# Moving the gate jobs of ScalarE, the gate stores and the gate loads in a two-layer transformer trunk

## The chip, the cores and the metric

The kernel runs on one core of a Trainium2 chip. The metric is the device time of one launch in microseconds (us); before the change it is 4043.3 us, the median of three runs (4035.92 to 4045.26).

## The reference

Two identical layers run one after the other on 512 tokens of width 1024: four sequence mixers and an output projection, a cross-attention to 256 memory tokens, and PEER, a mixture of 16384 tiny experts. The change touches PEER alone:

```python
q = (h @ w_query).reshape(B, L, PEER_HEADS, 2, PEER_HALF)
s = einsum('blhtd,htnd->blhtn', q, sub_keys)             # 8 heads, two sets of 128 keys
s1, i1 = top_k(s[..., 0, :], 16); s2, i2 = top_k(s[..., 1, :], 16)
top_s, pos = top_k(all 256 sums s1 + s2, 16)              # 16 experts per head: 128 per token
idx = i1 * 128 + i2 of those;  gate = softmax(top_s)
a = gelu(einsum('tkd,td->tk', u_tab[idx], h))
out = einsum('tk,tkd->td', gate * a, v_tab[idx])
```

## The kernel before

Each layer first runs the mixers, the cross-attention and the PEER scores; then `peer_experts` does the experts. The first 128 tokens (tile 0) gather their own rows of the two tables by indirect DMA. For the other 384 tokens (tiles t = 1, 2, 3) the kernel computes all 16384 experts densely, in 128 chunks of 128 experts, and multiplies by a gate matrix that is zero except where an expert was chosen. There are two loops over the chunks.

**The u loop** runs over chunks n = 0 to 127. SP loads the 512 KB of u for chunk n (`load_u`, three slots, ahead by the semaphore `u_split`). ScalarE rounds it to a high part (`round_u`, L1748), GpSimd makes the low part (`split_u`, L1844). TensorE multiplies (`experts`, L2076, 24 matmuls into one of two PSUM banks). ScalarE applies gelu (`gelu`, L1758), and in the same routine rounds u of chunk n+3 and stores the result of chunk n-1 to the DRAM tensor `acts` on its own DMA queue (`store_act`, L1752).

**The gates** of a tile t are made inside this loop, in the 16 chunks from START[t] = 34, 69, 104; these chunks are called spread chunks here. VectorE first routes the tile (`route(t)`: the top-k searches, with dot products of tile 0 filled in). Then come 32 jobs of four tokens, two jobs in each chunk. For a job VectorE makes two one-hot matrices (L2009, L2010, L2012, two buffers), TensorE multiplies them (`spread`, L2088, two PSUM banks in turn), and ScalarE copies the bank into an SBUF stage (`evict`, L1780). In a spread chunk TensorE's order is job, half of the 24 expert matmuls, job, the other half. Before job n it waits until ScalarE has copied job n-2 (`staged`). ScalarE copies both jobs of a chunk behind that chunk's `gelu`, so behind the end of its expert matmuls. VectorE makes the matrices of job n only when TensorE is done with job n-2 (`g_done`). TensorE starts chunk START[t]-1 only when the routing of tile t has ended (`sel_ready`).

The stage has two halves of 32 tokens. Each half is stored to the DRAM tensor `gates` in eight pieces of 16 chunks, 512 KB each (`store_gates`, L1769), which ScalarE issues on its DMA queue: those of half 0 at every second job in the second half of the 16 chunks, those of half 1 one per chunk behind them. As a partition holds 64 tokens of a chunk side by side and `gates` is laid out by chunk, a piece is 2048 runs of 256 bytes.

The dot products of tile 0 take their rows from six slots, which GpSimd fills by indirect DMA (`gather_row`, L1850, 512 KB each) between its `split_u` instructions, at chunks that a small planner (`gather_after`) writes out by hand.

**The v loop** runs over the same chunks again: SP loads v (512 KB), `acts` and `gates` (192 KB each) for a chunk, four slots each. VectorE multiplies act by gate (`gate`, L2027), ScalarE rounds (L1794, L1790), VectorE makes the low parts (L2032, L2037), TensorE does 18 matmuls into six banks (L2111). VectorE also adds up the gathered values of tile 0 (L2045, L2048), which GpSimd gathers into the space of stage half 1 (L1857) once the last stores of that half have landed. The first eight chunks are written out, the others run in a loop of eight chunks a turn.

Of the kernel before, what the change touches and what calls it, by code (L numbers as in the profile page):

```python
# [29 lines left out]
P = 128  # L30
# [1535 lines left out]
def peer_experts(k, hh_, hl_, scores, gates, acts, ring):  # L1566
# [16 lines left out]
    RING = 4  # L1583
    BODY = 8
# [5 lines left out]
    v_loaded, act_loaded, g_loaded = k.sems[41:45], k.sems[45:49], k.sems[49:53]  # L1590
    row_got, value_got = k.sems[53:59], k.sems[59:67]
    with ExitStack() as c:
        def sb(name, shape, dt=F32):
# [20 lines left out]
        a_in, g_in = (stages[:, 0, half_v + n * RING * SEQ:half_v + (n + 1) * RING * SEQ].rearrange("p (r t) -> p r t", r=RING)[:, :, 0:DENSE]  # L1614
                      for n in range(2))
# [22 lines left out]
        def job(t, q):  # L1638

            return (t - 1) * JOBS + q  # L1640
# [42 lines left out]

        with nc.Block() as block:
            @block.sync
            def _(e):
# [4 lines left out]
                def load_u(n):  # L1691
                    if n >= 2 + U_SLOTS:
                        e.wait_ge(u_split, n - U_SLOTS - 1)
                    e.dma_start(u[:, n % U_SLOTS, :, :], ut[n]).then_inc(u_loaded[n % U_SLOTS], 16)
# [5 lines left out]
                def load_gated(turn, n):  # L1700
                    s, at = n % RING, turn * BODY + n
                    e.dma_start(a_in[:, s, :], acts[bass.ds(at, 1)].rearrange("o p n -> p (o n)")).then_inc(act_loaded[s], 16)  # L1702
                    e.dma_start(g_in[:, s, :], gates[bass.ds(at, 1)].rearrange("o p n -> p (o n)")).then_inc(g_loaded[s], 16)

                def chunk(turn, n):
                    at = turn * BODY + n
                    e.wait_ge(v_split, at - RING + 1)
                    load_value(turn, n)
                    e.wait_ge(act_split, at - RING + 1)
                    load_gated(turn, n)  # L1710
# [7 lines left out]
                for n in range(5, NKEY):  # L1718
                    for t in (2, 3):
                        if n == (20 if t == 2 else START[3] - 30):  # L1720
                            e.wait_ge(sel_ready, 1 if t == 2 else 3)
                            load_scores(t)
                    load_u(n)
                e.wait_ge(stored[0], 16 * (PIECES - 1) * (TT - 1))
# [3 lines left out]
                e.wait_ge(stored_first[1], 16 * (TT - 1))  # L1728
                for n in range(RING):
                    e.wait_ge(a_stored[n], 16)  # L1730
                    load_gated(0, n)
# [3 lines left out]
                for n in range(RING, BODY):  # L1735
                    chunk(0, n)
                with e.Fori(0, TURNS - 1) as turn:
                    for n in range(BODY):
                        chunk(turn, BODY + n)

            @block.scalar
            def _(e):
# [20 lines left out]

                def store_gates(t, half, piece):

                    some = slice(piece * NKEY // PIECES, (piece + 1) * NKEY // PIECES)
                    at = (t - 1) * P + half * HALF
                    e.wait_ge(staged, job(t, 0) + (half + 1) * JOBS // 2)
                    e.dma_start(gates[some, :, at:at + HALF].rearrange("c p t -> p c t"),  # L1769
                                stage[half][:, some, :]).then_inc(stored[half] if piece else stored_first[half], 16)  # L1770
# [32 lines left out]
                for n in range(NKEY):  # L1803
                    if n == NKEY - 2:
                        e.wait_ge(dotted, KK)
                        e.activation(weights[:, :], dots[:, :], ACT.Gelu_apprx_tanh).then_inc(raised, 1)
                    gelu(n)
                    if n == 12:
                        exp_gates(0)
                    for t in range(1, TT):  # L1810
                        if n == START[t] - 5:
                            exp_gates(t)
                        for q in range(JOBS):
                            if START[t] + (STEPS * (q + 1) - 1) // KT == n:
                                evict(t, q)
                                if q >= JOBS // 2 and q % 2 == 1:
                                    store_gates(t, 0, (q - JOBS // 2) // 2)
                        piece = n - START[t] - JOBS * STEPS // KT
                        if 0 <= piece < PIECES:
                            store_gates(t, 1, piece)  # L1820
                    if n >= NKEY - 2:
                        round_value(0, n - NKEY + 2)
# [57 lines left out]
            def _(e):  # L1880
# [142 lines left out]
                def gate(n):  # L2023
                    s = n % RING
                    e.wait_ge(act_loaded[s], landed(0, n))
                    e.wait_ge(g_loaded[s], landed(0, n))  # L2026
                    e.tensor_tensor(a_in[:, s, :], a_in[:, s, :], g_in[:, s, :], ALU.mult).then_inc(gated, 1)  # L2027
# [239 lines left out]
def scratch_of(nc):  # L2267
    return {n: nc.dram_tensor(n, shape, F32).ap() for n, shape in
            (("scores", (TT, P, 2 * PH, NKEY)), ("gates", (NKEY, NKEY, SEQ - P)), ("acts", (NKEY, P, SEQ - P)), ("memory", (P, KT, MEM)))}
# [73 lines left out]
```

## Time and profile before

| | |
|---|---|
| median of the runs | 4043.3 us |
| the profiled execution | 4064.89 us, span 4063.1 us |
| TensorE busy, matmuls (17778) | 3636.7 us, 90% |
| VectorE / GpSimd / ScalarE busy | 2637.9 / 1658.2 / 1403.6 us |
| mean granted TensorE clock | 0.943 of full speed |
| DMA | 858.49 MB, mean 211 GB/s |

The profile is one execution, so it is compared with its own time; the median of the runs is 21.6 us below it. The span is cut into 40 slices of some 100 us. In layer 0 the u loop runs from about 680 to 1496 us and the v loop from there to 2033 us; in layer 1 from about 2697 to 3515 us and to 4054 us. The matmul engine's digits are 7 to 9 nearly everywhere; inside the u loop they change between 9 and 7.

### The profile page before, as it was taken

The numbers are of one execution on the slowest core, as the hardware profiler recorded it, in microseconds if no ns is written. First come the engines' busy times: TensorE is split into PE (matmuls) and PEld (weight loads), VectorE is DVE, ScalarE is ACT, GpSimd is POOL, SyncE is SP. The second block draws the span as 40 slices with busy tenths as digits, with TensorE's granted clock in tenths as the row PEclk, the third lists the DMA queues.
The fourth block names the chain that finished last, engine by engine and source line by source line (L and its number), as shares of the span: only waits on it lengthen the run. The fifth ranks groups of instructions, "written<-read, shape, count | busy, mean of one in ns | idle before, by whom it ended". The sixth has DMA issues, their size and how long they took to land. (4 is left out here: it accounts for less than half of the span.)

```text
span 4063.1 us, 52955 instructions
## 1 busy us (share of the span) xinstructions
PE 3636.7 (90%) x17778; PEld 3158.1 (78%) x17778; DVE 2637.9 (65%) x5262; ACT 1403.6 (35%) x2400; POOL 1658.2 (41%) x1144
## 2 busy tenths in 40 slices
PE   7888999978879779999988899999788887899999
PEld 6467778978879778888873778789788787788887
DVE  7755512867768638888787544148676675388887
ACT  4254433322323223333332543333223232233332
POOL 4623334644646332222156143447455464322221
PEclk8999999988989889999999899999899898999999
DMA  4004225757769589999731132358487686899996
GB/s 138 25 24 136 68 81 174 255 176 235 270 198 310 180 257 389 353 354 354 258 108 33 42 112 65 85 182 276 164 253 247 202 288 196 282 375 354 354 352 245
DMA packets 513025, 858.49 MB, mean 211 GB/s; under 512 B 236577, under 2 KB 340385, under 8 KB 509345
## 3 DMA queue, kind: packets, MB, share of 16 engines
q1 hardware_dynamic: 204064, 486.56, 36.7%
q0 software_dynamic: 73728, 268.47, 17.2%
q10 hardware_dynamic: 235008, 100.69, 9.0%
q8 instruction: 114, 1.87, 0.2%
q14 instruction: 111, 0.90, 0.1%
HBM read 743.37 MB, written 112.20 MB: 211 GB/s over the span
## 5 line engine op out<-in xcount | busy, mean ns | idle before, releaser
L1844 POOL TENSOR_TENSOR t_ul<-t_u,t_uh 128x1024 fp32r<-128x1024 f32 x168 | 405.5, 2414 | 453.7 <-ACT t_uh L1748 453.1
L1857 POOL DMA_INDIRECT t_stages<-in_peer_v,t_idx x256 | 261.3, 1021 | 749.5 <-DVE pair L2048 702.1
L2076 PE MATMUL pair<-h_high,t_uh 128*128 128x384 f32 x1376 | 508.7, 370 | 44.2 <-ACT t_act L1758 24.2
L1758 ACT ACTIVATE t_act<-pair 128x384 f32<-128x384 f32 x256 | 125.8, 491 | 1133.5 <-PE pair L2076 1049.8
L2111 PE MATMUL pair<-t_v_early,t_ah 128*128 128x512 f32 x1536 | 478.2, 393 | 26.8 <-DVE t_v_early L2037 26.8
L2076 PE MATMUL pair<-h_low,t_uh 128*128 128x384 f32 x1376 | 492.8, 358 | 0.0
L2076 PE MATMUL pair<-h_high,t_ul 128*128 128x384 f32 x1376 | 491.3, 357 | 0.0
L2111 PE MATMUL pair<-h_high,t_ah 128*128 128x512 f32 x1536 | 472.8, 389 | 0.0
L2088 PE MATMUL pair<-t_second,t_first 128*128 128x128 f32 x1536 | 232.8, 299 | 181.1 <-ACT t_stages L1780 181.1
L2009 DVE TENSOR_TENSOR t_second<-iota,pair 128x512 f32<-128x512 f32 x192 | 131.9, 687 | 374.0 <-PE pair L2088 337.3
L2088 PEld LDWEIGHTS pair<-t_second,t_first 128*128 128x128 f32 x1536 | 211.4, 207 | 209.9 <-ACT t_stages L1780 209.9
L2111 PEld LDWEIGHTS pair<-t_v_early,t_ah 128*128 128x128 f32 x1536 | 290.9, 190 | 89.9 <-issue 29.4
L297 POOL TENSOR_TENSOR x_w_low<-x_w_raw,x_w_high 128x512 fp32r<-128x512 f32 x128 | 176.3, 1385 | 438.5 <-ACT x_w_high L290 233.2
L1900 DVE CUSTOM_DVE_ANT_0 t_rows<-t_rows,pair 128x1024 f32<-128x1024 f32 x256 | 308.8, 1211 | 52.6 <-DMA t_rows<-in_peer_rows,t_idx 52.6
L2111 PEld LDWEIGHTS pair<-h_high,t_ah 128*128 128x128 f32 x1536 | 288.3, 188 | 59.9
L2048 DVE SCALAR_TENSOR_TENSOR pair<-t_stages,t_weights,pair 128x1024 f32<-128x1024 f32 x254 | 325.3, 1281 | 0.0
L2076 PEld LDWEIGHTS pair<-h_high,t_uh 128*128 128x128 f32 x1376 | 285.1, 207 | 50.4 <-issue 43.2
L1844 POOL TENSOR_TENSOR h_low<-t_u,h_high 128x1024 fp32r<-128x1024 f32 x84 | 200.5, 2387 | 280.1 <-ACT h_high L1748 279.7
L2111 PE MATMUL pair<-t_v_early,t_al 128*128 128x512 f32 x768 | 301.3, 392 | 0.0
L2111 PE MATMUL pair<-h_high,t_al 128*128 128x512 f32 x768 | 298.8, 389 | 0.0
L2076 PEld LDWEIGHTS pair<-h_low,t_uh 128*128 128x128 f32 x1376 | 284.6, 207 | 0.0
L2076 PEld LDWEIGHTS pair<-h_high,t_ul 128*128 128x128 f32 x1376 | 283.0, 206 | 0.0
(425 smaller groups left out, 8216.2 us busy)
## 6 DMA issues: line engine op xcount, KB each, us to landing
t_u<-in_peer_u SPq DMA_DIRECT2D x256, 512.0 KB, 4.3
t_stages<-in_peer_v SPq DMA_DIRECT2D x256, 512.0 KB, 5.3
acts<-t_act ACTq DMA_DIRECT2D x256, 192.0 KB, 4.3
gates<-t_stages ACTq DMA_DIRECT2D x96, 512.0 KB, 7.4
t_stages<-acts SPq DMA_DIRECT2D x256, 192.0 KB, 5.3
t_stages<-gates SPq DMA_DIRECT2D x256, 192.0 KB, 5.6
p_w_raw<-in_peer_wq SPq DMA_DIRECT2D x64, 256.0 KB, 3.0
m_w_raw<-in_w_in SPq DMA_DIRECT2D x48, 256.0 KB, 2.7
```

Source lines behind the costliest of these rows:

```text
L297: e.tensor_tensor(self.low[:, i % self.SPLIT, 0:width], self.raw[:, i % self.RAW, 0:width], self.high[:, i % self.SPLIT, 0:width].bitcast( ...
L1758: e.activation(act[:, n % A_SLOTS, :], k.bank[n % 2][:, 0:DENSE], ACT.Gelu_apprx_tanh).then_inc(gelu_done, 1)
L1844: e.tensor_tensor(ul[n % U_SLOTS], u[:, n % U_SLOTS, :, :], uh[n % U_SLOTS].bitcast(F32), ALU.subtract).then_inc(u_split, 1)
L1857: e.indirect_dma_start(value_slot[j % V_SLOTS], None, v_rows, bass.IndirectOffsetOnAxis(ap=idx[:, j:j + 1], axis=0)).then_inc(value_got[j ...
L1900: e.tensor_tensor_reduce(out=slot, in0=slot, in1=h_own, scale=1.0, scalar=0.0, op0=ALU.mult, op1=ALU.add, accum_out=dots[:, j:j + 1]).then ...
L2009: e.tensor_tensor(second[:, s, :, :], keys, bcast(selT[1][:, some], 2, NKEY), ALU.is_equal).then_inc(second_ready, 1)
L2048: e.scalar_tensor_tensor(out=own_sum, in0=slot, scalar=w, in1=own_sum, op0=ALU.mult, op1=ALU.add).then_inc(added, 1)
L2076: mm = e.matmul(out, a[n % U_SLOTS][:, q, :], b[:, 1:TT, q, :], start=(q == 0 and m == 0), stop=(q == KT - 1 and m == 2))
L2088: mm = e.matmul(g_bank(n)[:, a * NKEY:(a + 1) * NKEY], first[:, q % 2, a, :], second[:, q % 2, a, :], start=True, stop=True)
L2111: mm = e.matmul(k.bank[2 * t + half][:, :], l[:, s, (t - 1) * P:t * P], r[s][:, half * 512:(half + 1) * 512], start=(begins and m == 0), s ...
```

## The change

- **ScalarE's order.** In a spread chunk the copies of the chunk's two jobs (`evict`) come ahead of its `gelu` instead of behind it. The chunk in which a job is copied is the same.
- **The gate stores** move from ScalarE's to SP's DMA queue, between the u loads. `store_after` says behind which u load a piece goes out: half 0 at START[t]+13 to START[t]+20, one per load; half 1 from START[t]+21 on, one at every second load, for t = 3 two per load.
- **The layout of `gates`** in DRAM becomes (32, 128, 1536): four chunks lie side by side for each partition, so that a piece is 512 runs of 1 KB.
- **The gate loads** of the v loop fetch four chunks at once (768 KB, 6 KB per partition) into one of two buffers. One buffer lies in the stage, the other in the u slots, free once the u loop is done with them. `gate` reads its chunk from there in six runs of 64 elements.

The core of the diff:

```diff
-                    e.dma_start(g_in[:, s, :], gates[bass.ds(at, 1)].rearrange("o p n -> p (o n)")).then_inc(g_loaded[s], 16)
+                def load_gates(turn, g):
+                    at = turn * (BODY // GROUP) + g
+                    e.dma_start(g_store[g % 2], gates[bass.ds(at, 1)].rearrange("o p n -> p (o n)")).then_inc(g_loaded[g % 2], 16)
+        def store_after(t, half, piece):
+            if half == 0:
+                return START[t] + 13 + piece
+            return START[t] + 21 + (2 * piece if t < TT - 1 else piece // 2)
...
-                def chunk(turn, n):
+                def chunk(turn, n, regroup):
                     at = turn * BODY + n
                     e.wait_ge(v_split, at - RING + 1)
                     load_value(turn, n)
                     e.wait_ge(act_split, at - RING + 1)
-                    load_gated(turn, n)
+                    load_act(turn, n)
+                    if n % GROUP == 0 and regroup:
+                        e.wait_ge(gated, at - GROUP)
+                        load_gates(turn, n // GROUP)
...
                     load_u(n)
+                    for t in range(1, TT):
+                        for half in range(2):
+                            for piece in range(PIECES):
+                                if n == store_after(t, half, piece):
+                                    store_gates(t, half, piece)
+                for piece in range(PIECES):
+                    if store_after(TT - 1, 1, piece) >= NKEY:
+                        store_gates(TT - 1, 1, piece)
...
                 e.wait_ge(stored_first[1], 16 * (TT - 1))
+                load_gates(0, 0)
                 for n in range(RING):
                     e.wait_ge(a_stored[n], 16)
-                    load_gated(0, n)
+                    load_act(0, n)
+                e.wait_ge(u_split, NKEY - 2)
+                load_gates(0, 1)
...
+                    for t in range(1, TT):
+                        for q in range(JOBS):
+                            if START[t] + STEPS * q // KT == n:
+                                evict(t, q)
                     gelu(n)
...
-                        for q in range(JOBS):
-                            if START[t] + (STEPS * (q + 1) - 1) // KT == n:
-                                evict(t, q)
-                                if q >= JOBS // 2 and q % 2 == 1:
-                                    store_gates(t, 0, (q - JOBS // 2) // 2)
-                        piece = n - START[t] - JOBS * STEPS // KT
-                        if 0 <= piece < PIECES:
-                            store_gates(t, 1, piece)
```

## Rows read from the trace of the kernel before

**Rows 1.** Who waited for ScalarE's copies, L1780: us, times.
```profile
  PE pair L2088: 181.1, 90
```
**Rows 2.** Timeline of ScalarE, first 16 spread chunks: start, duration, idle before.
```profile
845.53 0.49 ACT L1758 ACTIVATE t_act<-pair 128x384 f32<-128x384 f32 x1 [4.51 <-PE pair L2076]
845.92 1.05 ACT L1748 ACTIVATE t_uh<-t_u 128x1024 fp32r<-128x1024 f32 x1
...
988.07 0.49 ACT L1758 ACTIVATE t_act<-pair 128x384 f32<-128x384 f32 x1 [7.39 <-PE pair L2076]
...
992.23 0.49 ACT L1758 ACTIVATE t_act<-pair 128x384 f32<-128x384 f32 x1 [1.75 <-PE pair L2076]
```
**Rows 3.** The same around chunk 69, the first spread chunk of tile 2.
```profile
1075.15 0.49 ACT L1758 ACTIVATE t_act<-pair 128x384 f32<-128x384 f32 x1 [3.08 <-PE pair L2076]
...
1081.10 0.49 ACT L1758 ACTIVATE t_act<-pair 128x384 f32<-128x384 f32 x1 [4.51 <-PE pair L2076]
```
**Rows 4.** ScalarE and its queue behind spread chunks, layer 0, tiles 1 and 3.
```profile
996.39 0.49 ACT L1758 ACTIVATE t_act<-pair 128x384 f32<-128x384 f32 x1 [2.72 <-PE pair L2076]
996.49 4.34 ACTq L1752 DMA_DIRECT2D acts<-t_act  x1
...
1041.51 0.49 ACT L1758 ACTIVATE t_act<-pair 128x384 f32<-128x384 f32 x1 [0.82 <-PE pair L2076]
...
1476.15 0.49 ACT L1758 ACTIVATE t_act<-pair 128x384 f32<-128x384 f32 x1 [2.72 <-PE pair L2076]
...
1496.42 0.47 ACT L1758 ACTIVATE t_act<-pair 128x384 f32<-128x384 f32 x1
```
**Rows 5.** Stretches: length, busy PE, PEld, DVE, ACT, POOL, clock, DMA share, GB/s.
```profile
845.50:922.00 76.50, 59.29 (x320) 56.73 (x320) 44.73 (x74) 20.36 (x34) 29.34 (x19) 0.87 0.45 154
922.00:988.00 66.00, 53.03 (x281) 51.11 (x282) 41.62 (x105) 15.79 (x27) 26.02 (x17) 0.84 0.73 215
996.00:1041.00 45.00, 39.93 (x218) 38.69 (x217) 42.90 (x152) 12.96 (x18) 29.74 (x20) 0.96 1.09 354
...
1497.00:1560.00 63.00, 52.24 (x219) 42.26 (x220) 45.45 (x55) 22.51 (x30) 21.65 (x21) 0.92 0.99 370
1560.00:1990.00 430.00, 430.00 (x1899) 356.06 (x1898) 357.56 (x427) 156.18 (x212) 109.34 (x107) 1.00 1.00 358
```
**Rows 6.** DMA issues from 996 to 1041 us: count, KB, median us to landing.
```profile
t_u<-in_peer_u SPq DMA_DIRECT2D x9, 512.0 KB, 6.4
gates<-t_stages ACTq DMA_DIRECT2D x7, 512.0 KB, 7.9
...
t_rows<-in_peer_rows,t_idx POOLq DMA_INDIRECT x10, 7.1
```
**Rows 7.** The page's costliest groups: busy us, mean ns, idle before and releaser.
```profile
L1844 POOL TENSOR_TENSOR t_ul<-t_u,t_uh 128x1024 fp32r<-128x1024 f32 x168 | 405.5, 2414 | 453.7 <-ACT t_uh L1748 453.1
...
L2009 DVE TENSOR_TENSOR t_second<-iota,pair 128x512 f32<-128x512 f32 x192 | 131.9, 687 | 374.0 <-PE pair L2088 337.3
...
L1900 DVE CUSTOM_DVE_ANT_0 t_rows<-t_rows,pair 128x1024 f32<-128x1024 f32 x256 | 308.8, 1211 | 52.6 <-DMA t_rows<-in_peer_rows,t_idx 52.6
```
**Rows 8.** Timeline of VectorE: the routing of tile 2, and what follows it.
```profile
979.13 3.19 DVE L1918 MAX8 t_best<-t_s 128x8 f32<-128x128 f32 x16
...
1061.32 0.29 DVE L1992 TENSOR_REDUCE t_esum<-t_ex 128x8 f32<-128x128 f32 x1 [3.06 <-ACT t_ex L1786]
...
1061.88 0.32 DVE L1997 TENSOR_TENSOR t_sel<-t_ex,t_esum 128x128 f32<-128x128 f32 x1
1070.96 0.69 DVE L2009 TENSOR_TENSOR t_second<-iota,pair 128x512 f32<-128x512 f32 x1 [8.76 <-PE pair L2097]
```
**Rows 9.** First and last matmul of the v loop, layer 0; GpSimd's first value gather.
```profile
1503.09 1.19 PE L2111 MATMUL pair<-t_v_early,t_ah 128*128 128x512 f32 x2 [8.51 <-DVE t_v_early L2037]
...
2032.47 0.39 PE L2111 MATMUL pair<-h_high,t_al 128*128 128x512 f32 x1
...
1502.65 1.12 POOL L1857 DMA_INDIRECT t_stages<-in_peer_v,t_idx  x1 [17.05 <-DMA gates<-t_stages]
```
**Rows 10.** The page's DMA issues: the gate loads of the v loop.
```profile
t_stages<-gates SPq DMA_DIRECT2D x256, 192.0 KB, 5.6
```

More of the change, by code:

```diff
@@ L1583, in peer_experts @@
     RING = 4
+    GROUP = 4
     BODY = 8
@@ L1589, in peer_experts @@
     dotted, raised, weighed, added, chunk_done, bank_done, v_round, v_split, gated, act_round, act_split, base_loaded = k.sems[29:41]
-    v_loaded, act_loaded, g_loaded = k.sems[41:45], k.sems[45:49], k.sems[49:53]
+    v_loaded, act_loaded, g_loaded = k.sems[41:45], k.sems[45:49], k.sems[49:51]
     row_got, value_got = k.sems[53:59], k.sems[59:67]
@@ L1613, in peer_experts @@
         v = stages[:, 0, 0:half_v].rearrange("p (r d) -> p r d", r=RING)
-        a_in, g_in = (stages[:, 0, half_v + n * RING * SEQ:half_v + (n + 1) * RING * SEQ].rearrange("p (r t) -> p r t", r=RING)[:, :, 0:DENSE]
-                      for n in range(2))
+        a_in = stages[:, 0, half_v:half_v + RING * DENSE].rearrange("p (r t) -> p r t", r=RING)
+        g_store = [stages[:, 0, half_v + RING * DENSE:half_v + (RING + GROUP) * DENSE],
+                   ring[0][:, :, :, :].rearrange("p r k n -> p (r k n)")[:, 0:GROUP * DENSE]]
+        g_in = [store.rearrange("p (s c t) -> p s c t", s=2 * (TT - 1), c=GROUP) for store in g_store]
+        gate_rows = gates.rearrange("g p (s x) -> g p s x", s=2 * (TT - 1))
         with ExitStack() as until_values:
@@ L1698, in load_value, with load_act, store_gates @@
                      .then_inc(v_loaded[n % RING], 16)
-                def load_gated(turn, n):
+                def load_act(turn, n):
                     s, at = n % RING, turn * BODY + n
                     e.dma_start(a_in[:, s, :], acts[bass.ds(at, 1)].rearrange("o p n -> p (o n)")).then_inc(act_loaded[s], 16)
-                    e.dma_start(g_in[:, s, :], gates[bass.ds(at, 1)].rearrange("o p n -> p (o n)")).then_inc(g_loaded[s], 16)
-                def chunk(turn, n):
+                def load_gates(turn, g):
+                    at = turn * (BODY // GROUP) + g
+                    e.dma_start(g_store[g % 2], gates[bass.ds(at, 1)].rearrange("o p n -> p (o n)")).then_inc(g_loaded[g % 2], 16)
+                def store_gates(t, half, piece):
+                    each = NKEY // GROUP // PIECES
+                    e.wait_ge(staged, job(t, 0) + (half + 1) * JOBS // 2)
+                    e.dma_start(gate_rows[piece * each:(piece + 1) * each, :, 2 * (t - 1) + half, :].rearrange("g p x -> p g x"),
+                                stages[:, half, piece * NKEY // PIECES * HALF:(piece + 1) * NKEY // PIECES * HALF]
+                                .rearrange("p (g x) -> p g x", g=each)).then_inc(stored[half] if piece else stored_first[half], 16)
+                def chunk(turn, n, regroup):
                     at = turn * BODY + n
@@ L1735, in _ @@
                 for n in range(RING, BODY):
-                    chunk(0, n)
+                    chunk(0, n, False)
                 with e.Fori(0, TURNS - 1) as turn:
                     for n in range(BODY):
-                        chunk(turn, BODY + n)
+                        chunk(turn, BODY + n, True)
             @block.scalar
@@ L1762, in gelu @@
                         store_act(n - 1)
[L1764 to L1770, printed above, removed]
                 def evict(t, q):
@@ L2024, in gate @@
                     s = n % RING
+                    a = a_in[:, s, :].rearrange("p (s t) -> p s t", t=HALF)
                     e.wait_ge(act_loaded[s], landed(0, n))
-                    e.wait_ge(g_loaded[s], landed(0, n))
-                    e.tensor_tensor(a_in[:, s, :], a_in[:, s, :], g_in[:, s, :], ALU.mult).then_inc(gated, 1)
+                    e.wait_ge(g_loaded[n // GROUP % 2], 16 * (n // (2 * GROUP) + 1))
+                    e.tensor_tensor(a, a, g_in[n // GROUP % 2][:, :, n % GROUP, :], ALU.mult).then_inc(gated, 1)
                 def low(n):
@@ L2268, in scratch_of @@
     return {n: nc.dram_tensor(n, shape, F32).ap() for n, shape in
-            (("scores", (TT, P, 2 * PH, NKEY)), ("gates", (NKEY, NKEY, SEQ - P)), ("acts", (NKEY, P, SEQ - P)), ("memory", (P, KT, MEM)))}
+            (("scores", (TT, P, 2 * PH, NKEY)), ("gates", (NKEY // 4, P, 4 * (SEQ - P))), ("acts", (NKEY, P, SEQ - P)), ("memory", (P, KT, MEM)))}
 def constants():
```

## The prediction

> **What bounds the kernel now.** I read the page first: TensorE is busy 90% of the span, so what can be won is its waits and the time it spends at the lower of its two clock levels (1.2 instead of 2.4 GHz). The list of who waited for whom names one wait that repeats: TensorE's spread matmuls stood idle until ScalarE's copy, L1780, 90 times, 181.1 us in all [rows 1]. There are 96 spread chunks, so this is about 2.0 us in nearly each. The timeline of ScalarE then gives the length of a chunk, from gelu to gelu. Outside the stretches it is 992.23 - 988.07 = 4.16 us [rows 2]. Inside, chunks 35 to 49 take 988.07 - 845.53 = 142.54 us, or 9.50 us each [rows 2]. But the first chunk of a stretch, which does the same two jobs and 24 expert matmuls, has nothing queued ahead of its first job, and takes 1081.10 - 1075.15 = 5.95 us [rows 3]. The 3.55 us between them are the wait of 2.0 and, for the rest, slow matmuls: in the stretches the mean granted clock is 0.84 to 0.87, in the v loop 1.00 [rows 5]. So each wait is followed by matmuls at 1.2 GHz, and both go together. Two smaller losses follow from the stores. Behind a stretch ScalarE's own issues block: the store of `acts` at 996.49 takes 4.34 us to issue, and chunks 52 to 60 take 1041.51 - 996.39 = 45.12 us where nine free ones take 37.44 [rows 4]. At the start of the v loop the value gather waits 17.05 us for the last gate stores, and the v loop takes 2032.47 + 0.23 - 1503.09 = 529.6 us where 128 chunks at 4.08 us take 522.2 [rows 9]; the 4.08 are 430 us of matmuls without a gap at full clock, which hold 105.4 chunks (1899 rows of matmuls at 18 a chunk) [rows 5].
>
> **The change, part by part.**
>
> *Copies ahead of gelu.* Job n of TensorE needs the copy of job n-2, which in the new order stands in the chunk before it, ahead of that chunk's gelu, and needs nothing but its own job's matmuls. What is queued behind the copies on ScalarE is gelu, the rounding of u three chunks ahead and the act store: the second copy starts in mid-chunk, gelu only at the end, so they are delayed by nothing. The wait goes, and with it the slow clock: 15 chunks x 3.55 = 53.3 us per stretch, x 6 stretches (they differ little) = 320 us. What is late next? VectorE: in the first stretch it is busy 44.73 us in 76.50, which is 8.05 chunks at 9.50, so 5.56 us per chunk [rows 5]. That is under 5.95, by little. Then the rows of the dot products: a gather stands behind a split of u, that behind the rounding, that behind a gelu, and by the hand-written plan the tightest row is needed three chunks later. The loop is gelu 0.49, rounding 1.05 [rows 2], split 2.41 [rows 7], two gather issues at 1.12 [rows 9], landing, a dot 1.21 and three one-hots at 0.69 [rows 7], some 1 us of hand-overs: 9.5 plus the landing. With 7.1 us, the landing under the heaviest load [rows 6], this is 16.6 us in three chunks, 5.5 us per chunk: still under 5.95. Bounds: 0 lost, or 6.5 - 5.95 = 0.55 us per chunk if rows land in 10 us (50 us in 90 chunks). I take 0.1 us, 9 us in all, nearest to the row. Gain 311 us.
>
> *Stores on SP's queue, spread, in 1 KB runs.* ScalarE's issue block goes: 7.7 us [rows 4] in each of four stretches, and 1496.42 - 1476.15 - 4 x 4.16 = 3.6 us [rows 4] behind each of the two last ones, 38 us. SP is in order, so a store whose `staged` is not reached would hold up the u loads. SP issues load n+1 when the split of chunk n-2 is done, near the start of chunk n-3: half 0, out behind load START+13, goes at about START+9, a chunk and a half after its last copy; half 1, behind load START+21, at about START+17, one chunk after. Neither waits. A u load has two chunks, over 8 us, from its issue to its rounding, and lands in 6.4 [rows 6]; a piece ahead of it on the queue adds 0.52 MB at 370 GB/s [rows 5], 1.4 us. That fits, and a late rounding has one more chunk of cover before TensorE sees it. The bytes: in chunks START+9 to +16 u 0.52, acts 0.20, one and a half rows 0.79, a piece 0.52 MB make 2.03 MB in 5.95 us, 341 GB/s. In START+17 to +20 the sum is 1.71 MB (half a piece, 1.4 rows) in 4.16 us, 412 GB/s, above the 370 that the trace sustains over 63 us [rows 5]: 4.63 - 4.16 = 0.5 us too much for four chunks, 2 us, which the prefetch mostly covers; after that one row per chunk makes 362 GB/s. Bounds for all this: nothing lost, or all 38 us still lost with another 38 on top. I take 5 us of stalls left and 3 for the burst: gain 30 us. With the old stores a piece went out every 5.0 us (nine chunks, 45.12 us) [rows 4]; that is the bound for a piece that is no cheaper.
>
> *Routing of tiles 2 and 3.* VectorE has less time for it, since the stretch before ends sooner. It now runs from 979.13 to 1062.20 and TensorE asks for it 8.76 us later [rows 8]. Of the 83.07 us 3.06 is a wait for ScalarE's exponential, because VectorE is early [rows 8]; 80.0 remain, with some waits for rows in them. In the new order VectorE can begin job 31 when job 29's matmuls are over, 8 us before the end of the stretch, and needs 3 for it (three one-hots and a dot [rows 7]); the routing begins about 5 us before chunk START+16, and 18 chunks of 4.16 follow until TensorE asks: 80 us. It just fits. Bounds: 0, or 3 us and as much again of slow clock, four times (24 us). I take 4 us lost.
>
> *Start of the v loop.* From the last gelu to the first v matmul it takes 1503.09 - 1496.42 = 6.7 us, in which ScalarE's issues block; gelu 0.47 [rows 4], a rounding of v as long as u's 1.05 [rows 2], one of act as long as a gelu, VectorE's low parts of act and of v (at most 0.69 and 1.21 by its instructions of those sizes [rows 7]) make 3.9, with hand-overs some 4.2. Another 7.4 us go inside the loop. The last stores now go out in three chunks and some 8 us after, so that the gather can begin about when GpSimd's last split is done, four or five chunks sooner; but the v loads, the 768 KB of gates and eight gathers then want the DMA together. Bounds: minus 5 (gates land late by their extra 0.59 MB twice), plus 2 x 9.9 = 20. I take 2.5 + 4 per layer: 13 us.
>
> *Gates for four chunks.* The bytes are the same. The load for chunks 4g to 4g+3 goes out with the act load of chunk 4g, over 12 us ahead of its use, and lands in 5.6 [rows 10] plus 0.59 MB at 358 GB/s [rows 5], 1.6: hidden by five us. `gate` reads runs of 64 elements instead of a row; VectorE has 430 - 357.6 us [rows 5] to spare, 0.69 per chunk; at twice its length the instruction would add at most that (0.69 is what 128x512 takes [rows 7]). I cost it at nothing, with that bound. The matmuls that fill the v loop stay.
>
> **The sum.** 311 + 30 - 4 + 13 = 350 us less, against the profiled execution 4064.9 - 350 = 3714.9 us; the median of the runs lies 21.6 us lower, so 3693 us.
>
> **The rivals.**
> - *Rows arrive too late.* Rows landing in 8.5 to 12 us under 341 GB/s would set the chunk at 6.0 to 7.2 us and push the routing late as well: 10 us gives 6.5, and with the routing's upper bound 3693 + 41 + 20 = 3754 us; 12 us some 3815. For it: only 0.4 us of spare per chunk, and VectorE near its limit as well. Against: 7.1 us at 354 GB/s [rows 6].
> - *u behind the stores.* If a piece takes SP's queue 5.0 us as before [rows 4], a chunk of START+9 to +16 takes 5.0 + 1.4 = 6.4 us: 0.45 x 48 = 22 us, and eight pieces in the last three chunks some 25 us per layer: 3765 us. Against: a quarter of the runs.
> - *The DMA ceiling.* If not the 370 GB/s of 63 us but the 358 GB/s of the v loop's 430 us [rows 5] is all that loads and stores together get, u loads fall behind after each stretch: 1.71 MB take 4.78 us, 0.6 too much in four chunks, the next ten lose 0.05 each, four times; and the eight pieces at the end of the loop cost some 2.5 us per layer. That is 17 us instead of my 3: 3707 us. For it: the v loop runs at that rate at a DMA share of 1.00. Against: its matmuls fill it, so it asks for no more, and the 63 us before it got 370 at a share of 0.99. The Trainium skill ("DMA: Bandwidth & Descriptors", Specifications) puts what HBM gives one core at about 358 GB/s, and so takes this rival's side. By that rule the 63 us at 370 could not stand; where the two differ, the measurement decides, so the rival gets little.
> - *The change does not unblock TensorE* because the copy still comes late (a job's one-hots come late instead): only 30 + 13 remain, 4000 us. Against: the first chunk of each stretch at 5.95.
> - *The gate loads come into the open, and it is slower than before.* If the 768 KB load were issued only when its chunk is due (a buffer released late), each of the 30 loads of the turns would show its 7.2 us in both layers: 432 us, 4125 us in all. It decides from 350 / 60 = 5.8 us per load on. Against: the release is by `gated`, four chunks back, which is passed before the act load ahead of it.
>
> **How the numbers follow.** My forecast, 3660 to 3725 us, has 0.64; the DMA ceiling 0.08, late rows 0.15, u behind the stores 0.08, no unblocking 0.02, gate loads in the open 0.03. The predicted time is 3693 us. The range 3660 (nothing lost anywhere: 320 + 38 + 20 = 378) to 3790 (rows landing in 10 us, with a share of the store queue's loss) holds 0.85. A change under 0.2% cannot be told from none here; faster by more than that has 0.96, within it 0.01, slower 0.03.
>
> **What would show it.** In the profile after: the idle time in front of the spread matmuls put down to L1780 gone; gelu to gelu 5.95 to 6.1 us through the stretches, at a clock near 1.00; no ScalarE issue over 1 us behind them; a routing that ends within some 3 us of TensorE's asking; the v loop still 4.08 us per chunk. The prediction is wrong if spread chunks take over 6.5 us, if the chunks behind them stay above 4.5, or if the v loop shows a gap every four chunks.

## The result and the profile after

The changed kernel takes 3699.5 us (median of four runs, 3677.36 to 3707.5) where the kernel before took 4040.5 beside it (four runs, 4035.92 to 4045.26): a ratio of 0.9147, 95% interval 0.9103 to 0.9191. The forecast was 3693.

The profiled execution of after took 3677.36 us (span 3675.6, mean clock 0.977), the lowest of its runs, while the one of before (4064.89) lies above all of its runs. So the two profiles differ by 387.5 us and the medians by 341. Where the 387.5 went is read by taking the time of every gelu of both traces:

| us | before | after | change | forecast |
|---|---|---|---|---|
| 90 spread chunks (without the first of each stretch) | 852.5 | 535.2 | -317.3 | -311 |
| 16, 16 and 8 chunks behind the stretches, both layers | 376.1 | 333.7 | -42.4 | -30 |
| chunk 33, both layers | 25.3 | 9.4 | -15.9 | none |
| last gelu to end of the last v matmul, layer 0 / 1 | 536.4 / 539.5 | 534.3 / 534.6 | -7.1 | -13 |
| chunks 68 and 103, both layers | 18.1 | 18.9 | +0.8 | +4 |
| chunks 19 to 23, both layers | 64.0 | 67.4 | +3.4 | none |
| mixers and the rest, untouched by the diff | | | -9 | none |

The last rows and chunk 33 change from run to run (below).

From the page of after: busy time, and the digits of TensorE's clock.

```profile
PE 3476.4 (95%) x17778; PEld 3033.6 (83%) x17778; DVE 2635.7 (72%) x5262; ACT 1413.5 (38%) x2400; POOL 1657.2 (45%) x1144
...
PEclk9989999999999999999989999999999999999999
```

The list of waits of after (engine, tile, line, released by: us, times, longest us):

```profile
ACT t_stages L1807 <- PE pair L2112: 186.1, 96, 1.9
...
DVE t_second L2032 <- PE pair L2112: 34.4, 38, 1.1
```

The wait of [rows 1] is no longer in it. It has turned round: ScalarE's copy (now L1807) waits for TensorE's spread matmuls (L2112), 1.9 us each time, and VectorE waits for TensorE as well. In a spread chunk the other engines now wait for the matmuls.

The timeline of ScalarE in the first stretch, and of VectorE at the end of the routing of tile 2 (start, duration, idle before):

```profile
843.55 0.49 ACT L1793 ACTIVATE t_act<-pair 128x384 f32<-128x384 f32 x1 [1.48 <-PE pair L2100]
...
844.88 0.59 ACT L1807 ACTIVATE t_stages<-pair 128x512 f32<-128x512 f32 x1
847.41 0.60 ACT L1807 ACTIVATE t_stages<-pair 128x512 f32<-128x512 f32 x1 [1.94 <-PE pair L2112]
849.50 0.49 ACT L1793 ACTIVATE t_act<-pair 128x384 f32<-128x384 f32 x1 [1.48 <-PE pair L2100]
...
926.80 0.49 ACT L1793 ACTIVATE t_act<-pair 128x384 f32<-128x384 f32 x1 [1.48 <-PE pair L2100]
...
930.96 0.49 ACT L1793 ACTIVATE t_act<-pair 128x384 f32<-128x384 f32 x1 [2.72 <-PE pair L2100]
...
999.69 1.90 DVE L2020 TENSOR_TENSOR t_sel<-t_ex,t_esum 128x128 f32<-128x128 f32 x1
1002.23 0.69 DVE L2032 TENSOR_TENSOR t_second<-iota,pair 128x512 f32<-128x512 f32 x1 [0.64 <-PE pair L2121]
```

Gelu to gelu a spread chunk now takes 849.50 - 843.55 = 5.95 us, what only the first one of a stretch took before [rows 3]. The first chunk behind the stretch takes 930.96 - 926.80 = 4.16.

Windows of after, columns as in [rows 5]: the first stretch, the chunks behind it, the start of the v loop, its middle.

```profile
837.60:926.80 89.20, 89.20 (x602) 89.20 (x601) 79.92 (x145) 37.86 (x60) 55.66 (x36) 1.00 0.82 278
926.80:1001.00 74.20, 74.20 (x430) 74.20 (x429) 74.03 (x262) 28.95 (x39) 60.92 (x37) 1.00 1.02 374
...
1310.00:1380.00 70.00, 61.00 (x259) 50.32 (x260) 57.28 (x70) 25.98 (x36) 18.31 (x19) 0.93 1.02 394
1380.00:1800.00 420.00, 420.00 (x1855) 347.89 (x1854) 347.47 (x413) 151.53 (x207) 104.31 (x104) 1.00 0.97 355
```

TensorE is busy without a gap through stretch and chunks behind it, at clock 1.00 where [rows 5] had 0.84 to 0.96. VectorE has 79.92 of 89.20 us in the stretch: 5.3 us of each 5.95, the narrow fit that was reckoned. Only the start of the v loop shows gaps.

### The profile page after: what moved, and what is told of

It reads as the page before. It is cut to its first block and busy times, and to the rows that moved or that the text cites. A ratio compares the mean times of both kernels' runs of the same rounds, so it can differ in the third digit from the quotient of the medians.

```text
span 3675.6 us, 52671 instructions
## 1 busy us (share of the span) xinstructions
PE 3476.4 (95%) x17778; PEld 3033.6 (83%) x17778; DVE 2635.7 (72%) x5262; ACT 1413.5 (38%) x2400; POOL 1657.2 (45%) x1144
## 5 line engine op out<-in xcount | busy, mean ns | idle before, releaser
L2100 PE MATMUL pair<-h_high,t_uh 128*128 128x384 f32 x1376 | 474.1, 345 | 20.5 <-PEq L119 11.8
L2100 PE MATMUL pair<-h_low,t_uh 128*128 128x384 f32 x1376 | 462.5, 336 | 0.0
L2100 PE MATMUL pair<-h_high,t_ul 128*128 128x384 f32 x1376 | 462.2, 336 | 0.0
L1923 DVE CUSTOM_DVE_ANT_0 t_rows<-t_rows,pair 128x1024 f32<-128x1024 f32 x256 | 309.4, 1214 | 50.8 <-DMA t_rows<-in_peer_rows,t_idx 50.6
L2100 PEld LDWEIGHTS pair<-h_high,t_uh 128*128 128x128 f32 x1376 | 260.8, 190 | 22.4 <-issue 12.1
L1873 POOL DMA_INDIRECT t_rows<-in_peer_rows,t_idx x256 | 245.5, 959 | 73.9 <-issue 28.5
L2100 PEld LDWEIGHTS pair<-h_low,t_uh 128*128 128x128 f32 x1376 | 260.9, 190 | 0.0
L2100 PEld LDWEIGHTS pair<-h_high,t_ul 128*128 128x128 f32 x1376 | 260.2, 189 | 0.0
L1817 ACT ACTIVATE h_high<-t_stages 128x1024 fp32r<-128x1024 f32 x128 | 135.9, 1062 | 320.5 <-PE pair L2135 165.1
L1817 ACT ACTIVATE t_v_early<-t_stages 128x1024 fp32r<-128x1024 f32 x128 | 136.1, 1063 | 318.2 <-PE pair L2135 157.4
```

Of the source, the lines that this page charges most:

```text
L1817: e.activation(vh[n % RING], v[:, n % RING, :], ACT.Copy).then_inc(v_round, 1)
L1873: e.indirect_dma_start(row_slot[j % R_SLOTS], None, u_rows, bass.IndirectOffsetOnAxis(ap=idx[:, j:j + 1], axis=0)).then_inc(row_got[j % R_ ...
L1923: e.tensor_tensor_reduce(out=slot, in0=slot, in1=h_own, scale=1.0, scalar=0.0, op0=ALU.mult, op1=ALU.add, accum_out=dots[:, j:j + 1]).then ...
L2100: mm = e.matmul(out, a[n % U_SLOTS][:, q, :], b[:, 1:TT, q, :], start=(q == 0 and m == 0), stop=(q == KT - 1 and m == 2))
```

## The experiments

Each ran beside the kernel before. "Order" means the copies ahead of gelu.

**e1_order_only**: the kernel before with the order alone.

```diff
...
+                            if START[t] + STEPS * q // KT == n:
+                                evict(t, q)
                     gelu(n)
...
-                                evict(t, q)
                                 if q >= JOBS // 2 and q % 2 == 1:
                                     store_gates(t, 0, (q - JOBS // 2) // 2)
```

> Only ScalarE's order is changed: the copies of a spread chunk's two jobs come ahead of its gelu; the gate stores (256-byte runs) stay on ScalarE's queue at their old places, the gate loads stay one per chunk. My theory (the wait for the copies and the slow clock behind it are one loss of 3.5 us in 90 chunks): spread chunks 5.95 us, the blocked issues of ScalarE behind the stretches stay (some 43 us), the late value gather stays (7 us): 3750 us. Rival (the old stores need the old slow pace): with chunks of 5.95 us ScalarE's queue falls behind already in the second half of a stretch, chunks there take 7 us or more: 3800 us or more.

Measured: 3737.7 us, ratio 0.9234 [0.92, 0.9268], 304 us less than before. All spread chunks take 5.95. The 16 chunks behind a stretch take 73.8 to 78.7 us in place of 66.6, because ScalarE's own issues block, as the timeline of its queue in e1 shows (start, duration of the issue):

```profile
934.66 3.73 ACTq L1752 DMA_DIRECT2D acts<-t_act  x1
...
939.82 6.67 ACTq L1752 DMA_DIRECT2D acts<-t_act  x1
...
947.19 4.58 ACTq L1752 DMA_DIRECT2D acts<-t_act  x1
```

So the order is nine tenths of the gain, and cures nothing of what the stores cost.

**e2_stores_only**: the changed kernel with the copies behind gelu again.

> All of the change but ScalarE's order: the copies stay behind gelu. My theory: spread chunks stay at 9.4 us, chunks behind them fall to 4.16 (43 us less), the start of v gains some 7: 3990 us. Rival (the stores' move carries a part of what the order seemed to bring, through DMA load in the stretches): under 3900 us.

Measured: 4002.8 us, ratio 0.9894 [0.9858, 0.993]: 39 us less than before. 304 + 39 = 343 beside the whole change's 341: the parts add up, as far as medians tell whose intervals are some 15 us to either side. The 39 hold the start of the v loop too, since e2 leaves out the order alone. The wait for L1807 is back, and so is the slow clock (the waits of e2, then its window 846 to 988 us):

```profile
PE pair L2111 <- ACT t_stages L1807: 181.1, 90, 2.0
```

```profile
846.00:988.00 142.00, 113.82 (x624) 109.35 (x623) 90.79 (x216) 38.09 (x64) 59.77 (x39) 0.88 0.57 189
```

Behind the stretches the chunks take 333.7 us in all, as in after: 4.16 us each, but for one of 4.38 in every 16.

**e5_filled_wait**: what part of the 3.55 us per chunk is the wait, and what the clock? To the kernel before, 20 matmuls of 128x128 are added ahead of a chunk's first job, so that TensorE works where it waited.

```diff
+                    if q and q % 2 == 0:
+                        at = START[t] + q // 2
+                        e.wait_ge(gelu_done, at - 1)
+                        for _ in range(20):
+                            e.matmul(k.bank[at % 2][:, DENSE:DENSE + P], hh_[:, 1, 0, :], hh_[:, 1, 0, :], start=True, stop=True)
                     if n >= 2:
                         e.wait_ge(staged, n - 1)
```

> The kernel before, with 20 small matmuls (128x128) on TensorE ahead of the first job of each spread chunk but the first, where it waits for the copy; their results go to columns that nothing reads. The wait for the copy stays. My theory (the idle time ahead of the copy brings the lower clock, which makes the next matmuls slow): the granted clock in the stretches goes to about 1.00 and chunks of 9.8 us become 8.3, the wait itself stays: 4040 - 90 x 1.2 = 3930 us. Rival (the slow matmuls have another cause, such as the copies' own traffic): the clock stays at 0.85, the time at 4040 us or above.

Measured: 3937.0 us beside 4051.9 before, ratio 0.972 [0.9696, 0.9745]: more work, 115 us less. The window 846 to 988 us of e5, then the timeline of its ScalarE and TensorE in one chunk:

```profile
846.00:988.00 142.00, 142.00 (x1003) 142.00 (x1003) 103.38 (x271) 41.59 (x69) 70.79 (x46) 1.00 0.69 223
```

```profile
852.95 0.49 ACT L1758 ACTIVATE t_act<-pair 128x384 f32<-128x384 f32 x1 [5.83 <-PE pair L2076]
...
861.19 0.49 ACT L1758 ACTIVATE t_act<-pair 128x384 f32<-128x384 f32 x1 [5.83 <-PE pair L2076]
...
860.99 2.35 PE L2088 MATMUL pair<-h_high 128*128 128x128 f32 x20
```

The clock is 1.00 and every chunk takes 861.19 - 852.95 = 8.24 us. Against 5.95 the filled wait is 2.29 us; the remaining 9.50 - 8.24 = 1.26 us of a chunk [rows 2] were matmuls at 1.2 GHz behind an idle TensorE, 1.26 x 90 = 113 us of the measured 115 (111 between the two profiles). (By the clock of [rows 5], 0.84 to 0.87, an estimate of the work lost is 0.145 x 9.50 = 1.4 us per chunk.) So the lower clock comes from the idle time, and the prediction's 3.55 is 2.29 + 1.26. The time before is uneven in just this way. Two of its chunks, one behind the other, from gelu to gelu (columns as in [rows 5]):

```profile
855.35:865.14 9.79, 7.78 (x40) 7.46 (x40) 6.03 (x11) 2.41 (x4) 4.25 (x3) 0.83 0.49 177
865.14:873.38 8.24, 6.23 (x40) 5.91 (x40) 4.91 (x9) 2.41 (x4) 3.32 (x2) 1.00 0.47 149
```

TensorE idles 2.01 us in both, and in every one of the 90 chunks. In 70 of them the mean clock is 0.83 and the chunk takes 9.8 us; in the other 20 it stays at 1.00 and the chunk takes 8.2. So "each wait is followed by matmuls at 1.2 GHz" holds for 70 of 90; what sets the 20 apart the runs do not show.

**e3_256b_on_sp** and **e4_1kb_on_act**: the change to the stores has two parts, another queue and longer runs. With the order in both, e3 has the spread stores on SP but the old layout of 256-byte runs (and gate loads by chunk); e4 has the 1 KB runs and gate loads for four, but the stores at their old places on ScalarE's queue. (e3 thus changes the queue and the pace of the stores together.)

The core of e3 against after, in SP's program, and then of e4, out of SP's program and into ScalarE's:

```diff
...
-                    e.dma_start(gate_rows[piece * each:(piece + 1) * each, :, 2 * (t - 1) + half, :].rearrange("g p x -> p g x"),
+                    e.dma_start(gates[some, :, at:at + HALF].rearrange("c p t -> p c t"),
```

```diff
...
-                                if n == store_after(t, half, piece):
-                                    store_gates(t, half, piece)
...
+                        if 0 <= piece < PIECES:
+                            store_gates(t, 1, piece)
```

> The order and the move of the gate stores to SP's queue, spread as in the change, but with the old layout: 2048 runs of 256 bytes a piece, gate loads one per chunk. If the run length sets a piece's cost (5.0 us as on ScalarE's queue before), u loads queue behind the pieces: chunks START+9 to +16 take some 6.4 us and the end of the u loop loses 25 us per layer: 3770 us. If only the bytes count: 3700 us, as the full change.

> The order and the new layout (1 KB runs, gate loads for four chunks), but the stores stay on ScalarE's queue at their old places, one piece per chunk. If the number of runs made ScalarE's issue block: no blocked issues, 3700 us. If the queue or the pace of one piece per 4.16 us did it: ScalarE's issues block behind the stretches as before, 3740 us or more.

Measured: e3 takes 3705.1 us (0.9165 [0.9129, 0.9201]), e4 3699.8 us (0.9138 [0.9101, 0.9175]). The 16 chunks behind a stretch take 66.8 to 67.5 us in e3 and 66.8 to 68.3 in e4, so either part alone takes nearly all of the loss away: of the 42.4 us, 5.0 are left in e3 and 3.4 in e4, at most 2 per stretch. In e4 some issues still block, without TensorE seeing most of it. The first timeline is ScalarE's queue in e4, the second SP's in e3:

```profile
958.66 3.28 ACTq L1771 DMA_DIRECT2D acts<-t_act  x1
```

```profile
1298.11 9.92 SPq L1723 DMA_DIRECT2D gates<-t_stages  x4
1308.29 3.76 SPq L1703 DMA_DIRECT2D t_stages<-in_peer_v  x4
```

But the run length has its worth at the end of the u loop, where the stores stand close together: four short-run pieces hold SP for 9.92 us (2.5 each), four of 1 KB for 4.28 in after (1.1 each, below). The v loads stand behind them, and from the last gelu to the first v matmul e3 takes 15.0 and 14.5 us, after 9.4 and 9.8: 10 us for both layers. The whole times, which spread by 15 us and more, do not show it.

e4 shows the start of v from another side. Without gate stores on SP's queue its loads of act go out 17 us ahead of the last gelu instead of 9 to 10, the value gathers begin 6 us behind it instead of 7 to 8 ahead, and the first v matmul comes 4.2 and 4.4 us behind it. But TensorE waits another 4.3 to 4.6 us soon after, and to the end of the last v matmul it takes 536.1 and 536.4 us, no less than in after.

**e6_rows_later**: how much room is left for the rows? In the changed kernel all gathers of rows are planned one chunk later.

```diff
-            return 18 if j < R_SLOTS else math.ceil(times[j - R_SLOTS] + 1) + 2
+            return 18 if j < R_SLOTS else math.ceil(times[j - R_SLOTS] + 1) + 3
```

> The changed kernel with every row gather behind the first six one chunk later in GpSimd's order. My loop of gelu, rounding, split, gathers, landing, dot and one-hots (9.5 us plus a landing of 5 to 7) then has two chunks instead of three: spread chunks of 7.3 to 8.2 us, 3820 to 3900 us. If rows have more room than I reckoned: chunks stay at 5.95, 3700 us.

Measured: 3805.1 us (two runs), ratio 0.9395 [0.9378, 0.9412], 106 us more than the changed kernel run again beside it. The page's row of the dot products in e6, then in after:

```profile
L1923 DVE CUSTOM_DVE_ANT_0 t_rows<-t_rows,pair 128x1024 f32<-128x1024 f32 x256 | 309.6, 1214 | 174.5 <-DMA t_rows<-in_peer_rows,t_idx 174.2
```

```profile
L1923 DVE CUSTOM_DVE_ANT_0 t_rows<-t_rows,pair 128x1024 f32<-128x1024 f32 x256 | 309.4, 1214 | 50.8 <-DMA t_rows<-in_peer_rows,t_idx 50.6
```

VectorE's wait for rows grows from 50.6 to 174.2 us. The spread chunks go to 6.4 to 6.5 us in the mean for tiles 1 and 2 and to 8.0 to 8.1 for tile 3, where most stay at 5.95 and about every third takes 9.7 to 14.1; this is 93 us over 5.95 in all. Chunks 68 and 103 (the wait for the routing) go from 4.7 to 10.4 and 11.2, 24 us. So the loop of the rival is real, and late rows do push the routing as well. It came in below the 3820 to 3900 expected: for tiles 1 and 2 the rows had more room than was reckoned. Why tile 3 fares worse was not looked into.

**after_again** (the changed kernel) and **e7_v_start**: the start of the v loop is the one term that came in at half of its forecast. In e7 SP brings the first act and gates ahead: the last stores of tile 3 one chunk sooner, then v 0, v 1, gates, act 0, act 1, and so on.

```diff
...
                 for n in range(RING):
                     load_value(0, n)
+                    if n == 1:
+                        e.wait_ge(stored_first[1], 16 * (TT - 1))
+                        load_gates(0, 0)
+                        for s in range(2):
+                            e.wait_ge(a_stored[s], 16)
+                            load_act(0, s)
...
```

> The changed kernel again, to have it beside e7 on one chip and to see a second profile. 3693 to 3707 us; spread chunks 5.95 us in every stretch. If the 24 us by which its profiled execution beat the sum in stretches that the change does not touch come and go by run, the wait ahead of chunk 33 (8 us per layer before, none in the profile after) and the mixers (7 us) differ from that profile again.

> The changed kernel with two moves at the start of v: the last eight gate stores one chunk earlier, and SP's loads in the order of need (v of chunks 0 and 1, the four-chunk gates, act 0 and 1, then v and act of 2 and 3). My theory (the first v matmul waits for act 0, which queues behind four v loads and the gates): from the last gelu to the first v matmul 5 instead of 9.4 us, 3690 us. Rival (the value gathers fill the DMA, so the order of the loads does not matter): no change, 3700 us.

Measured: after_again 3698.7 us (0.9121 [0.9105, 0.9137]), e7 3694.2 (0.9125 [0.9112, 0.9137]): the whole times don't tell them apart, the stretch does. (In the profile of after_again the spread chunks are 5.95 again, but for one of 6.75; against the first profile of after chunk 33 took 15 us more and the mixers 9, so both do differ from run to run.) In e7 the first v matmul comes 3.73 us behind the last gelu in both layers, in after_again 9.33 and 9.83. But from the last gelu to the last v matmul it is 532.1 and 532.5 us, in after_again 534.1 and 534.2: two thirds of the 5.6 to 6.1 us are given back at chunk 4. From the timelines of TensorE, VectorE and SP in e7, and SP's list of waits there, 1300 to 1335 us:

```profile
1321.79 1.19 PE L2139 MATMUL pair<-t_v_early,t_ah 128*128 128x512 f32 x2 [3.77 <-DVE t_v_early L2065]
...
1338.31 0.82 PE L2139 MATMUL pair<-h_high,t_ah 128*128 128x512 f32 x2 [2.48 <-DVE h_high L2065]
...
1336.00 0.56 DVE L2055 TENSOR_TENSOR t_stages<-t_stages,t_u 128x384 f32<-128x384 f32 x1 [6.63 <-DMA t_stages<-acts]
...
1309.51 0.33 SPq L1716 DMA_DIRECT2D t_u<-gates  x1
1327.61 0.34 SPq L1707 DMA_DIRECT2D t_stages<-in_peer_v  x1
...
SPq L1772 <- DMA acts<-t_act: 17.4, 1, 17.4
```

SP stands idle from 1309.8 to 1327.6 us. Ahead of chunk 4 it waits until all 128 act stores have landed, and issues 9.55 us behind the last gelu (1318.06); in after it was 1319.08 - 1309.57 = 9.51. (The gate stores, for which it waits there too, had landed 11.4 us before that gelu in e7.) The loads then need 8 us, and TensorE waits.

**e8_act_early**: e7, but chunks 4 to 7 wait for their own act stores only.

```diff
...
-                for slot in range(A_SLOTS):
-                    e.wait_ge(a_stored[slot], 16 * (NKEY // A_SLOTS))
-                e.wait_ge(stored[1], 16 * (PIECES - 1) * (TT - 1))
                 for n in range(RING, BODY):
+                    e.wait_ge(a_stored[n % A_SLOTS], 16 * (n // A_SLOTS + 1))
                     chunk(0, n, False)
+                for slot in range(A_SLOTS):
+                    e.wait_ge(a_stored[slot], 16 * (NKEY // A_SLOTS))
+                e.wait_ge(stored[1], 16 * (PIECES - 1) * (TT - 1))
```

> On top of the kernel with the reordered v start: the loads of v and acts for chunks 4 to 7 of the v loop wait only for their own act stores (chunks 4 to 7 of the u loop, landed long ago) instead of for all 128, and the check that all stores have landed stands behind them. In the kernels so far SP issues the load of chunk 4 some 9.5 us after the last gelu (1318.06 to 1327.61; in the changed kernel 1309.57 to 1319.08), which fits the landing of the last act store. Theory (this wait bounds the start of the v loop, whatever is done ahead of it): the first loads of the loop go out some 6 us sooner, the 2.48 us wait of TensorE at the sixth chunk half goes with its slow clock; from the last gelu to the last v matmul 528 us instead of 532.1 and 532.4, so some 8 us less than the reordered kernel's 3694: 3686, to be read from the stretch itself, as single runs differ by 15 us. Rival (bytes: values, acts, gates and eight gathers ask for more than the DMA gives, which is at a share of 1.00 there): the loads go out sooner and land later, the stretch stays at 532 us and the time at 3694.

Measured: 3683.8 us (3669.66 to 3693.84, five runs), ratio 0.9094 [0.9072, 0.9116] beside 4051.3 before. From the last gelu to the last v matmul it is 529.2 us in both layers; the theory said 528, the rival 532. SP and TensorE in e8:

```profile
1320.96 0.34 SPq L1707 DMA_DIRECT2D t_stages<-in_peer_v  x1
...
1335.88 0.70 PE L2140 MATMUL pair<-h_high,t_ah 128*128 128x512 f32 x2 [1.08 <-DVE h_high L2066]
```

The load goes out 3.8 us behind the last gelu (1317.16), when the first v slot comes free, and the wait of TensorE is down to 1.08 us. The stretch is 4.9 us per layer shorter than in after_again, 10 in all; the medians differ by 15, with intervals that overlap a little, so the 10 are what is shown. e8 has the lowest median of these versions.

## Why the prediction was right, point by point

- *Copies ahead of gelu*, forecast 311 us: right in mechanism and size. 317 between the profiles, 304 in e1's medians. A chunk is 5.95 as the first one of a stretch had shown; the loss of 9 us for late rows did not come, and VectorE, "under 5.95, by little", waits for TensorE (34.4 us in all). e5 shows that the wait and the clock went as one, though the lower clock came in 70 of the 90 chunks. The reckoning of the rows has a slip: its terms add up to 10.5 us ahead of the landing, not 9.5, since the hand-overs were left out. With 7.1 for the landing that is 5.9 us per chunk, 0.1 under 5.95 and not 0.4. That nothing was lost agrees with e6, where the rows of tiles 1 and 2 had more room than either sum leaves, but this sum had not shown it.
- *Stores on SP*, forecast 30: 42.4 between the profiles (e2's 39 hold the start of v as well). The block went whole, and it was 42.4 us and not 38, because the 7.7 us of one stretch were taken for four that lost 7.7 to 10.2. The 8 us set aside for stalls and the burst were not needed: the chunks behind a stretch ran 74.2 us at 374 GB/s with TensorE at 100%.
- *Routing of tiles 2 and 3*, forecast 4 lost: 0.8. It ends at 999.69 + 1.90 = 1001.59 us, and chunk 68 takes 4.72 us where it took 4.52. It just fits, as reckoned.
- *Start of the v loop*, forecast 13 gained: 7.1. This step was mis-sized, and its first half had the wrong sign: the gap from gelu to the first v matmul was to fall from 6.7 to 4.2 us and rose to 9.4 and 9.8. SP, GpSimd, VectorE and TensorE in after:

```profile
1289.08 4.28 SPq L1722 DMA_DIRECT2D gates<-t_stages  x4
1293.63 5.11 SPq L1707 DMA_DIRECT2D t_stages<-in_peer_v  x4
1298.79 1.49 SPq L1716 DMA_DIRECT2D t_stages<-gates  x1
1300.33 1.92 SPq L1712 DMA_DIRECT2D t_stages<-acts  x4
...
1302.77 0.95 POOL L1880 DMA_INDIRECT t_stages<-in_peer_v,t_idx  x1 [1.78 <-DMA gates<-t_stages]
...
1314.48 0.56 DVE L2051 TENSOR_TENSOR t_stages<-t_stages 128x384 f32<-128x384 f32 x1 [12.19 <-DMA t_stages<-acts]
...
1319.00 1.19 PE L2135 MATMUL pair<-t_v_early,t_ah 128*128 128x512 f32 x2 [9.47 <-DVE t_v_early L2061]
```

  The value gather did come sooner, with 1.78 us of waiting in place of 17.05 [rows 9], and inside the loop 4.9 and 8.1 us were won. But the first acts stand on SP's queue behind four stores, four v loads and the 768 KB of gates, and act 0 landed some 14 us after its issue, when the gathers had joined. The prediction named the right transfers ("want the DMA together") and had their delay in its lower bound, but took none for the first chunk in its sum. That SP also waits for the last act store ahead of chunk 4 was not seen; e7 and e8 show it.
- *Gates for four chunks*, forecast nothing: in the loop's 420 us TensorE has no gap, 1855 matmul rows or 4.08 us a chunk. The loads land in 8.1 us (forecast 7.2), well inside four chunks, and the multiply by the gate, in six runs of 64, takes 0.56 us (1314.48 above). From the page:

```profile
t_stages<-gates SPq DMA_DIRECT2D x32, 768.0 KB, 8.1
```

- *The sum*: between the profiles 387 us, 37 more than forecast; between the medians 341, 9 less. The profile of before stood 24 us above its median, that of after 22 below, so it is partly luck that the correction by 21.6 us brought the forecast from 3714.9 to within 7 us of the median: it explains nothing. Of the profiles' surplus of 37 us, 25 are chunk 33 and the mixers, which the change does not touch. Three small slips change nothing: 1899 rows at 18 are 105.5 chunks, not 105.4; the last matmul of the v loop takes 0.39 us in its row, not 0.23; and 378 us less make 3665, not 3660.
- *The rivals.* Late rows: real (e6), but not reached. u behind the stores: not here; its price of 5.0 us per piece was the pace of ScalarE's blocked queue. On SP, in e3, a short-run piece takes 0.43 to 1.5 us of issue where the pieces are spread, and 2.0 to 2.5 where they follow each other in the last three chunks. The DMA ceiling: falls. 374 GB/s for 74 us and 394 for 70 us stand above its 358. The Trainium skill ("DMA: Bandwidth & Descriptors", Specifications) gives about 358 GB/s, too, as HBM's limit for a core, half of what it gives for a stack; this kernel runs on one core alone, and here the measurement decides. No unblocking and gate loads in the open: not seen.

## What to carry to other kernels

Where a repeated wait of the busiest engine is short, ask what runs slower behind it: here 2.3 us of waiting cost 3.55, and filling the wait with useless matmuls alone won 115 us. A job that frees a buffer belongs ahead of one on the same engine whose input comes later, when its own is ready in mid-chunk. When loads are moved to a phase change, put the first chunk's small loads first and let each load wait for its own data, not for all of it.

## What was not expected of the hardware

**Some VectorE instructions stand still while GpSimd splits.** Chunk 33, where TensorE waits for the routing of tile 1, took 4.71 us in the first profile of after and 13.13 and 11.27 in after_again, the same kernel: 15 of the 21 us between their spans. The tail of that routing in after_again (VectorE, GpSimd, ScalarE), then in after:

```profile
806.81 2.68 DVE L1988 TENSOR_SCALAR t_row<-t_pos 128x128 uint32<-128x128 uint32 x1
...
832.51 2.30 DVE L2020 TENSOR_TENSOR t_sel<-t_ex,t_esum 128x128 f32<-128x128 f32 x1
...
806.98 2.42 POOL L1867 TENSOR_TENSOR h_low<-t_u,h_high 128x1024 fp32r<-128x1024 f32 x1
...
832.30 2.35 POOL L1867 TENSOR_TENSOR h_low<-t_u,h_high 128x1024 fp32r<-128x1024 f32 x1
...
828.72 0.49 ACT L1793 ACTIVATE t_act<-pair 128x384 f32<-128x384 f32 x1 [2.72 <-PE pair L2100]
...
841.85 0.49 ACT L1793 ACTIVATE t_act<-pair 128x384 f32<-128x384 f32 x1 [11.69 <-PE pair L2100]
```

```profile
801.88 0.23 DVE L1988 TENSOR_SCALAR t_row<-t_pos 128x128 uint32<-128x128 uint32 x1
...
799.34 2.62 POOL L1867 TENSOR_TENSOR t_ul<-t_u,t_uh 128x1024 fp32r<-128x1024 f32 x1 [0.66 <-ACT t_uh L1783]
...
803.50 2.39 POOL L1867 TENSOR_TENSOR h_low<-t_u,h_high 128x1024 fp32r<-128x1024 f32 x1 [0.43 <-ACT h_high L1783]
```

L1988 takes 0.23 us when it falls between two splits, and 2.68 when a split starts beside it; both then end together (809.49 and 809.40). L2020, 2.30 us, lies inside a split. The eleven profiles hold 88 runs of L2020's instruction: the six that lie clear of every split take 0.29 us, and the 82 that begin inside one end 0.14 to 0.16 us behind its end, wherever they began, so they take 0.3 to 2.4 us. The routing ended 6.1 us behind the gelu of chunk 32 in after_again (832.51 + 2.30 - 828.72), in after 0.1 ahead of it; from the exponential's input on, the same instructions took 31.0 and 27.4 us, which is 3.6 of the 6.2; where the other 2.6 come from was not looked into. The rest of chunk 33's loss goes with TensorE's clock, which is 0.74 and 0.85 in the mean of chunk 33 in after_again and 1.00 in the chunks beside it. Chunk 33 follows L1988 without exception: in the six layers of the eleven profiles in which L1988 of tile 1 took 0.21 to 0.24 us, chunk 33 takes 4.7 us, and in the 16 in which it took 2.66 to 2.69, 11.3 to 14.8. The Trainium skill ("SBUF — State Buffer", section "SBUF: two separate sides") has VectorE and GpSimd share a pair of ports, locked for a whole instruction, which VectorE needs in its two-port modes or with two operands in SBUF. L2020 has two such operands, and agrees; whether L1988 runs in such a mode no row shows. The dot products, which have one operand in PSUM, take 1.21 us beside a split and clear of one. No experiment moved the splits away, so the cause rests on the regularity of the rows, and that of chunk 33's length on two things that go together. It may be a part of why single runs of the changed kernel spread by up to 30 us; effects under 15 us were therefore read from stretches.

**Gate stores on a queue can hold up its engine's next issue.** In e1 the act stores behind a stretch take 3.7 to 6.7 us to issue in the lines above, where they take 0.34 on a free queue. On ScalarE's queue it took both many short runs and a fast pace: with a piece of 2048 runs per 4.16 us the issues block; with one per 5.95 us, inside the stretches of e1, they take 0.34 us (41 of 42), and with pieces of 512 runs per 4.16 us mostly 0.34 and at most 3.7 (e4). What the other queue does by itself stays open, since e3 also spread the stores.
